# An encoder layer on one core: order of loads and of the first chunks in the front, and of the first two MLP jobs

## What is computed

```
mod = silu(c) @ w_mod + b_mod            # shift1, scale1, gate1, shift2, scale2, gate2
h = rms_norm(x, g_mix) * (1.0 + scale1) + shift1
z = h @ w_in
...                                      # Fourier mixer, gated recurrence, output projection
x = x + gate1 * mix
h = rms_norm(x, g_mlp) * (1.0 + scale2) + shift2
ff = square(relu(h @ w_ff1)) @ w_ff2
x = x + gate2 * ff                       # then a last rms_norm
```

## Time and profile before

| | |
|---|---|
| time, median of 3 runs | 1424.35 us (1422.76 to 1425.23) |
| the profiled execution's own time | 1427.07 us |
| its span, first to last instruction | 1425.3 us |
| TensorE busy | 1392.2 us, 98% of the span |
| TensorE's first matmul | 14.03 us |
| mean granted clock | 0.993 |

### The profile page before, as it was taken

One profiled execution on the slowest core, in us unless ns is written; L12 is line 12 of the kernel. 1 busy time (PEld: TensorE's weight loads), 2 busy tenths in 40 slices (PEclk: granted clock), 3 DMA queues, 4 the chain that ended last, 5 costly groups with the idle time before them and its releaser, 6 DMA issues.

```text
span 1425.3 us, 18554 instructions
## 1 busy us (share of the span) xinstructions
PE 1392.2 (98%) x7594; PEld 1183.4 (83%) x7594; DVE 807.9 (57%) x771; ACT 592.1 (42%) x719; POOL 472.8 (33%) x269
## 2 busy tenths in 40 slices
PE   4999999999999999999999999999999999999998
PEld 2776778898888788888888888888888888888887
DVE  4967688795438954454533454353656434344584
ACT  6667979665335632232222223232332222433241
POOL 0011102135003764565455454532232222233131
PEclk9999999999999999999999999999999999999998
DMA  9443421105310343343343334479997444445542
GB/s 369 161 154 141 133 96 38 45 23 189 143 60 30 111 159 115 121 149 121 139 154 115 126 118 161 158 266 388 377 390 289 148 148 148 162 175 198 203 177 89
DMA packets 75702, 231.31 MB, mean 162 GB/s; under 512 B 5729, under 2 KB 9953, under 8 KB 66786
## 3 DMA queue, kind: packets, MB, share of 16 engines
q1 hardware_dynamic: 75618, 230.12, 44.1%
HBM read 165.09 MB, written 65.01 MB: 161 GB/s over the span
## 4 chain that ended last, share of the span: by engine, by line
PE 53%; issue 2%; POOL 1%; ACT 0%; POOLq 0%
PE bank L785 18%; PE bank L786 18%; PE bank L787 18%; POOL x L2483 0%; ACT w_hi L1579 0%; POOL w_lo L2460 0%; POOL w_s L2436 0%; PE bank L1099 0%; POOL w_lo L2452 0%; PE bank L1092 0%; POOLq L2491 0%; POOL x L2489 0%; POOLq L2488 0%; POOLq L2450 0%
## 5 line engine op out<-in xcount | busy, mean ns | idle before, releaser
L785 PE MATMUL bank<-hin_hi,w_lo 128*128 128x512 f32 (+1 forms) x896 | 302.4, 338 | 0.0
L786 PE MATMUL bank<-hin_lo,w_hi 128*128 128x512 f32 (+1 forms) x896 | 302.0, 337 | 0.0
L787 PE MATMUL bank<-hin_hi,w_hi 128*128 128x512 f32 (+1 forms) x896 | 301.4, 336 | 0.0
L2218 DVE TENSOR_TENSOR hin_lo<-hin,hin_hi 128x3072 fp32r<-128x3072 f32 x28 | 138.9, 4963 | 201.8 <-ACT hin_hi L1591 201.8
L2460 POOL TENSOR_TENSOR w_lo<-w_raw,w_hi 128x2048 fp32r<-128x2048 f32 x28 | 129.6, 4628 | 327.6 <-ACT w_hi L1579 326.1
L785 PEld LDWEIGHTS bank<-hin_hi,w_lo 128*128 128x128 f32 x896 | 170.2, 190 | 18.4 <-issue 0.2
L786 PEld LDWEIGHTS bank<-hin_lo,w_hi 128*128 128x128 f32 x896 | 170.3, 190 | 17.8 <-issue 0.2
L787 PEld LDWEIGHTS bank<-hin_hi,w_hi 128*128 128x128 f32 x896 | 170.1, 190 | 17.8
L1579 ACT ACTIVATE w_hi<-w_raw 128x2048 fp32r<-128x2048 f32 x28 | 53.6, 1916 | 290.3 <-PE bank L787 184.6
L2452 POOL TENSOR_TENSOR w_lo<-w_raw,w_hi 128x512 fp32r<-128x512 f32 x51 | 73.8, 1447 | 200.1 <-ACT w_hi L1517 200.1
L1526 ACT ACTIVATE hid<-bank 128x768 f32<-128x768 f32 (+2 forms) x68 | 52.5, 772 | 163.3 <-PE bank L787 162.5
(11 more groups left out here) (293 smaller groups left out, 3110.8 us busy)
## 6 DMA issues: line engine op xcount, KB each, us to landing
hin<-hid_all SPq DMA_DIRECT2D x28, 1536.0 KB, 6.6
hid_all<-hid SPq DMA_DIRECT2D x105, 384.0 KB, 2.5
w_raw<-in_w_ff SPq DMA_DIRECT2D x36, 1024.0 KB, 8.9
w_raw<-in_w_ff SPq DMA_DIRECT2D x68, 256.0 KB, 2.9
mod_raw<-in_w_mod SPq DMA_DIRECT2D x16, 1024.0 KB, 5.3
x<-in_xT SPq DMA_DIRECT2D x5, 2048.0 KB, 13.4
w_sums<-w_raw SPq DMA_DIRECT2D x8, 1024.0 KB, 14.9
w_raw<-w_sums SPq DMA_DIRECT2D x8, 1024.0 KB, 10.3
```

The costliest lines, as they stand in the source:

```text
L785: pe.matmul(out, w_lo, v_hi, start=first, stop=False, skip_group_check=True)
L786: pe.matmul(out, w_hi, v_lo, start=False, stop=False, skip_group_check=True)
L787: return pe.matmul(out, w_hi, v_hi, start=False, stop=last, skip_group_check=True)
L2218: dve.tensor_tensor(hin_lo[n % 3][:].rearrange("p t n -> p (t n)"), hin[n % 3][:].rearrange("p t n -> p (t n)"), hin_hi[n % 3][:].rearrang ...
```

## The change

In the front, the two w_in tiles and the first modulation quarter are loaded ahead of chunk 1, which now comes in two halves, and the third quarter is loaded ahead of chunk 2. ACT and DVE split the two weight tiles ahead of the root of chunk 0. The squares of chunk 1 move behind `copy_rstd(0)`. TensorE does `front(0, 0)` ahead of everything of chunk 1, and `mod_quarter(2)` behind `front(0, 1)` instead of ahead of it.

In the MLP, two `hid` tiles are exchanged from job 0's last step on (`hid_tile`), so that the copy of P1 of job 1 waits neither for step T1 nor for a store. Steps C22 and C12 of job 0 stand earlier on DVE. The ReLU and square of C12 go from DVE (step B12) to ACT. `split_w1_hi(1, P7)` and `split_w1_hi(1, P3)` stand ahead of `token_hi(P7, 1)` and `token_hi(P4, 1)`.

```diff
+    def hid_tile(j, q):
+
+        if j == S_T4:
+            return hid[S_B11]
+        return hid[S_T4] if j == S_B11 and q else hid[j]
...
-        load_chunk(1)
-        load_first(0)
         sp.dma_start(win_raw[:], w_in_d[TILES[0]]).then_inc(ld_win, 16)
         sp.dma_start(win_raw1[:], w_in_d[TILES[1]]).then_inc(ld_wg, 16)
+        load_first(0)
+        for h, s in enumerate((ld_x[1], ld_x1)):
+            rows = xT_d[h * FT * P:(h + 1) * FT * P, CH:2 * CH]
+            sp.dma_start(x[:, 1, h * FT:(h + 1) * FT, :], rows.rearrange("(k p) n -> p k n", p=P)).then_inc(s, 16)
         load_first(1)
+        load_first(2)
         load_chunk(2)
-        load_first(2)
         load_first(3)
...
         pe.wait_ge(vec_dve, 2)
+        mod_quarter(0)
         norm_spread(0)
-        mod_quarter(0)
         mod_quarter_sum(0)
+        front(0, 0)
         norm_sum(1)
         mod_quarter(1)
         norm_spread(1)
-        front(0, 0)
         mod_quarter_sum(1)
         front(1, 0)
+        front(0, 1)
         mod_quarter(2)
-        front(0, 1)
         mod_quarter_sum(2)
         front(1, 1)
...
             square(0, k)
+        split_win_hi(0)
+        split_win_hi(1)
+        root(0)
+        diagonals(0)
+        mod_copy(0)
+        copy_rstd(0)
         for k in range(2):
             square(1, k)
-        root(0)
-        square(1, 2)
-        diagonals(0)
-        for k in range(3, KD):
+        front_hi(0, 0)
+        for k in range(2, KD):
             square(1, k)
-        split_win_hi(0)
-        split_win_hi(1)
-        mod_copy(0)
-        copy_rstd(0)
         root(1)
-        front_hi(0, 0)
...
             act.wait_ge(ff1_mm, 7 * q + i + 1)
-            after(act, hid_step, NHID * (q - 1) + step)
-            after(act, st_hid[j], 16 * q)
+            if q > 1 or i != P1:
+                after(act, hid_step, NHID * (q - 1) + step)
+                after(act, st_hid[j], 16 * q)
...
         split_w1_hi(1, P6)
         first_relu_square(S_B11, B11, 1)
-        token_hi(P6, 1)
-        split_w1_hi(1, P2)
-        first_relu_square(S_B22, B22, 3)
-        token_hi(P2, 1)
+        first_relu_square(S_T3, B12, 3)
         ff1_out(0, P4, S_B21, T4)
-        token_hi(P3, 1)
         for q in range(1, NJ):
             ff1_out(q, P1, S_B11, T1)
             if q == 1:
+                token_hi(P6, 1)
+                split_w1_hi(1, P2)
+                first_relu_square(S_B22, B22, 5)
+                token_hi(P2, 1)
+                token_hi(P3, 1)
+                split_w1_hi(1, P7)
+                split_w1_hi(1, P3)
                 token_hi(P7, 1)
                 token_hi(P4, 1)
...
         add_squares(0)
-        rstd(0)
-        add_squares(1)
         split_win_lo(0)
         split_win_lo(1)
+        rstd(0)
         mod_quarter_columns(0)
         front_scale(0, 0)
+        add_squares(1, range(1))
+        front_lo(0, 0)
+        add_squares(1, range(1, KD - 1))
         rstd(1)
-        front_lo(0, 0)
...
         token_lo(P1, 1)
+        hid_out(0, C22)
+        hid_out(0, C12)
         token_sum(2, 1)
-        hid_out(0, C22)
         token_lo(P5, 1)
-        for step in (C12, B12, T1):
-            hid_out(0, step)
         token_sum(4, 1)
         token_lo(P6, 1)
-        token_sum(3, 1)
+        hid_out(0, T1)
         token_lo(P2, 1)
         hid_out(0, T3)
+        token_sum(3, 1)
         hid_out(0, T2)
         token_lo(P7, 1)
```

More of the change, by code:

```diff
@@ L371, in build_encoder @@
     ld_x0 = sem("ld_x0_rest")
+    ld_x1 = sem("ld_x1_rest")
     ld_sin = sem("ld_sin")
@@ L641, in store_hid @@
                 if q == 0 and step in (B11, B22):
-                    sp.wait_ge(first_relu, 2 if step == B11 else 4)
+                    sp.wait_ge(first_relu, 2 if step == B11 else 6)
             else:
                 sp.wait_ge(ff1_sq, q + 1)
-            sp.dma_start(hid_d[j, :, pair, c0:c1], hid[j][:, c0:c1]).then_inc(st_hid[j], 16)
+            sp.dma_start(hid_d[j, :, pair, c0:c1], hid_tile(j, q)[:, c0:c1]).then_inc(st_hid[j], 16)
         def w2_freed(m):
@@ L709, in _ @@
                 store_hid(q - 1, S_B21, 0)
-                store_hid(q - 1, S_T4, T4)
+                if q > 1:
+                    store_hid(q - 1, S_T4, T4)
             if q + 1 < NJ:
@@ L714, in _ @@
                 load_w1(q + 1, (A11, A21))
+                if q == 1:
+                    store_hid(0, S_T4, T4)
                 sp.wait_ge(w1_sum, 4 * q + 4)
@@ L1176, in square @@
             if n < NN:
-                act.wait_ge(ld_x0 if c == 0 and k >= FT else ld_x[c], 16)
+                if c < 2 and k >= FT:
+                    act.wait_ge((ld_x0, ld_x1)[c], 16)
+                else:
+                    act.wait_ge(ld_x[c], 16)
             else:
@@ L1523, in ff1_out @@
             act.wait_ge(ff1_mm, 7 * q + i + 1)
-            after(act, hid_step, NHID * (q - 1) + step)
-            after(act, st_hid[j], 16 * q)
-            act.activation(hid[j][:, c0:c1], ps[:, buf + c0:buf + c1], ACT.Relu if i == P4 else ACT.Copy
+            if q > 1 or i != P1:
+                after(act, hid_step, NHID * (q - 1) + step)
+                after(act, st_hid[j], 16 * q)
+            act.activation(hid_tile(j, q)[:, c0:c1], ps[:, buf + c0:buf + c1], ACT.Relu if i == P4 else ACT.Copy
                            ).then_inc(ff1_copy, 1)
@@ L1647, in _ @@
             if q == 1:
+                token_hi(P6, 1)
[5 more added lines that the diff above has]
+                split_w1_hi(1, P3)
                 token_hi(P7, 1)
                 token_hi(P4, 1)
-            split_w1_hi(q, P7)
-            split_w1_hi(q, P3)
+            else:
+                split_w1_hi(q, P7)
+                split_w1_hi(q, P3)
             ff1_out(q, P6, S_T3, T2)
             split_w1_hi(q, P4)
+            if q == 1:
+                ff1_out(q, P7, S_B22, T2)
             if q + 1 < NJ:
@@ L1658, in _ @@
                 split_hin_hi(0)
-            ff1_out(q, P7, S_B22, T2)
+            if q > 1:
+                ff1_out(q, P7, S_B22, T2)
             if q + 1 < NJ:
@@ L2145, in out_of @@
                 return ps[:, 2 * CH * buf + c0:2 * CH * buf + c1]
-            slot, at = hid, NHID * q
+            slot, at = [hid_tile(j, q) for j in range(7)], NHID * q
             if step == U2:
@@ L2169, in hid_out @@
                 if q == 0:
-                    dve.wait_ge(first_relu, 2)
+                    dve.wait_ge(first_relu, 4)
                 after(dve, st_hid[S_T1], 16 * q)
@@ L2175, in hid_out @@
                 if q == 0:
-                    dve.wait_ge(first_relu, 4)
+                    dve.wait_ge(first_relu, 6)
                 m = dve.tensor_tensor(slot[S_T3][:, cols], slot[S_B22][:, cols], slot[S_T3][:, cols], ALU.subtract)
@@ L2183, in hid_out @@
                 dve.wait_ge(ff1_sq, q + 1)
-                after(dve, st_hid[S_T4], 16 * q)
+                if q:
+                    dve.wait_ge(st_hid[S_T4], 16 * q)
+                else:
+                    dve.wait_ge(st_hid[S_B11], 16)
                 m = dve.tensor_tensor(slot[S_T4][:, cols], slot[S_B21][:, cols], slot[S_T2][:, cols], ALU.subtract)
-            m.then_inc(hid_step, 2 if q == 0 and step in (C11, C22) else 1)
+            m.then_inc(hid_step, 2 if q == 0 and step in (C11, C22, C12) else 1)
         def w1_add(q, i):
```

## The result

The changed kernel takes 1428.29 us (median of 15 runs, 1426.24 to 1431.53), the kernel before 1423.70 on the same chip (15 runs, 1422.15 to 1425.76). The ratio is 1.0032, 95% interval 1.0025 to 1.0039: slower by 4.6 us. The profiled execution took 1427.85 us, with a span of 1426.1. Two single runs were slow ones, one of `mlp_copy_first` (3416.73 us) and one of before beside it (2327.06): the ratios leave them out, and they move the printed medians by 0.1 us.

A forecast was written before the change was run, and what follows sets the result against it. TensorE, busy 98% of the span, bounds the kernel; only its idle time and low clock can change. Front +3.4 and MLP -2.4 give +1.0 us on a median of 1424.35: 1425.4, eight in ten within 1421.0 to 1428.6.

The forecast's parts named there:

- Term 1: Front: chunk 2's later landing and quarter 2's uncovered copy delay the sum of chunk 2, +3.4 us (2.3 to 6).
- The idle time ahead of `front(0, 1)`: Front: `front(1, 0)` done at 40.5, `front(0, 1)` starting at 42.1, so TensorE idles 1.6 us.
- The bound from above: Front: up to 6 us lost if idle time brings the low clock back to passes or a quarter on the chain.
- Rival B: Front loses +5.6 us: timed runs of before had less low clock, or new idle time brings it; 1427.6, chance 0.25.
- Term 2: MLP jobs 0 and 1: P7 of job 1 starts at 504.8 instead of 507.2, -2.4 us (0 to -6.5).
- The clock counted as unchanged: MLP: 2.4 us idle ahead of P7, as long as the 2.33 before, so the low clock behind it stays the same.
- Rival A: MLP stretch closes entirely: P7 starts at 502.4, clock stays high, -6.5 us there; 1421.2 in all, chance 0.17.
- Rival C: Front: `front(0, 0)` leads by 7 us and some 4 of them last; 1418, chance 0.06.
- The sum: Whole kernel: +3.4 - 2.4 = +1.0 us on the profiled execution of 1427.07; median forecast 1425.4.

The follow-up runs named there:

- `mlp_copy_first`: MLP half alone on before's front, plus ACT copying P6 of job 1 ahead of two roundings and DVE's T1, T3, T2 one place earlier; 1421.93 us, ratio 0.9971 to before.
- `front_quarter2`: Front half of the change alone, with modulation quarter 2 back ahead of `front(0, 1)`; 1426.46 us, ratio 1.0020 to before.
- `front_only_fill`: Front half of the change alone, with unused matmuls in TensorE's idle time ahead of `front(0, 0)` and `front(1, 0)`; 1429.33 us, ratio 1.0038 to before.
- The second profile: The kernel before, unedited, timed against itself and profiled again; 1425.29 us, ratio 0.9998.
- `mlp_only`: MLP half of the change alone, on the front of before; 1424.22 us, ratio 0.9997 to before.

## Why the prediction was right or wrong

**Term 1, the chain: right in its later steps.** The span after begins its work 0.63 us earlier (13.40 against 14.03). With that shift taken off (without it each forecast is 0.4 to 0.7 us late), the prediction has `front(1, 0)` at 37.0 (measured 37.16), `front(0, 1)` at 41.5 (41.52), quarter 2 at 44.4 (44.35), `front(1, 1)` at 48.3 (48.39) and the sum of chunk 2 at 52.1 (52.11). What it did not have is the half speed of `front(0, 0)` and `front(1, 0)`; the first product of chunk 0 came at 24.78, where it had about 26. The landing of chunk 2 is shown by ACT's first square in ACT's timeline after (it answers to the earlier trace rows):

```profile
37.77 2.19 ACT L1208 ACTIVATE sq<-x 128x512 f32<-128x512 f32 x4 [0.88 <-DMA x<-in_xT]
...
46.34 0.60 ACT L1253 ACTIVATE mod_row<-bank 128x512 f32<-128x512 f32 x1 [3.06 <-PE bank L836]
46.84 1.32 ACT L1261 ACTIVATE hi_f<-x,mod 128x512 fp32r<-128x512 f32 x2
...
504.83 1.06 ACT L1516 ACTIVATE hi_f<-h_f 128x1024 fp32r<-128x1024 f32 x1 [2.09 <-DVE h_f L2115]
505.79 1.04 ACT L1516 ACTIVATE t4b_hi<-t4b_s 128x1024 fp32r<-128x1024 f32 x1
506.74 0.79 ACT L1542 ACTIVATE hid<-bank 128x768 f32<-128x768 f32 x1
```

The forecast less the shift was 37.9. The rows at 46.34 and 46.84 are the uncovered copy and the rounding behind it: ACT waits 3.06 us for quarter 2. `front_quarter2` took that away and won 4.0 us of time, 2.7 by the ratios, and 1.9 in its profile's front.

**The idle time ahead of `front(0, 1)`: wrong.** I had 1.6 us there at the high clock. In the profile after there is none, since `front(1, 0)` ran mostly at 0.50. The bound from above named this case. It cost next to nothing on the chain here: the `lo` of chunk 2 is begun at 40.61, so by my estimate `front(0, 1)` could have started only 0.2 us sooner than its 41.52; `front_only_fill` shows the other side of it, where the clock is high and the wait is 2.14 us.

**Term 1 as a difference: too small.** This is the step that failed. I set the new chain against the one profile of before, whose quarter 1 was at 0.50 and whose front was 35.30 us long, and moved the result to the median of the runs. The second profile has 34.06, so the chain costs 4.7 us against it. Rival B gave exactly this reason, a shorter stretch at the low clock in the timed runs, and its time was 1427.6. The mean clock fits it: 0.994 to 0.996 in the runs of before that the ratios of the experiments use, 0.993 in the profile of before. The median came out at 1428.29, 0.7 above. The two slowest runs of after (1430.79 and 1431.53) have a mean clock of 0.991 against 0.993 for most, but so has one of 1428.30; they have no trace, so what made them slow is not shown.

**Term 2: the mechanism was right, the size only against one form of before.** P5 and P6 no longer wait. From U2 of job 0 to P7 of job 1 the profile before has 23.80 us (483.40 to 507.20), after 21.74 (486.15 to 507.89): 2.06 less, where I had 2.4. Against the other form, in which P7 starts 21.36 us after U2 with the MLP half of before, the changed half is 0.4 us later. I had the earlier trace rows with POOL's 4.83 us before me and took it as an upper bound for the changed kernel; that before itself can run without it, and then has nothing to give, I did not ask. The last three rows of ACT above are the two roundings and the copy of P6 ahead of P7. DVE's timeline after, in the same stretch, which answers to the earlier trace rows:

```profile
498.56 2.31 DVE L2127 TENSOR_TENSOR lo_r<-h_r,hi_r 128x1024 fp32r<-128x1024 f32 x1
500.79 1.77 DVE L2201 TENSOR_TENSOR hid<-hid,hid 128x512 f32<-128x512 f32 x1
502.49 2.30 DVE L2115 TENSOR_TENSOR h_f<-h_r,h_f 128x1024 f32<-128x1024 f32 x1
504.72 1.75 DVE L2204 TENSOR_TENSOR hid<-hid,hid 128x512 f32<-128x512 f32 x1
506.39 1.21 DVE L2127 TENSOR_TENSOR lo_f<-h_f,hi_f 128x1024 fp32r<-128x1024 f32 x1
```

DVE's operations take 2.3 and 1.8 us where they take 1.2 and 0.7 alone: the turns with POOL. `token_sum(3, 1)` ends at 504.79, ACT rounds twice and copies until 507.53, and P7 starts. The profile names `lo_f` as releaser, which ends at 507.60. The two end 0.07 us apart, so that row alone cannot tell which holds P7. `mlp_copy_first` moved both, the copy ahead of `token_sum(3, 1)` and P7's `lo` further back. There P7 starts at 501.97, and its `lo` is made only from 504.06: P7's first part does not need it (its second part waits for it, at 505.43), so in the profile after it was the copy. The Trainium skill, SBUF — State Buffer, section "Who interferes with whom", has the two engines exclude each other for a whole instruction. By that rule the trace agrees in this stretch; the row of 4.83 us in the earlier trace rows, in which POOL got nothing, did not come again in the profile after (its longest pair is 4.70 us for two). It stands in the five profiles of the second form above and in none of the four of the first.

**The clock counted as unchanged: wrong.** That is the second step that failed. I had 2.4 us of idle time ahead of P7; it was 3.12, and behind it the clock was low for 3.4 us in the profile after and 6.8 in `mlp_only`. The two groups of `mlp_only` show the price: the means are 1421.4 us (four runs, high clock) and 1424.7 (seven). Which stretch the faster four had at the high clock has no trace, so that it was this one is inferred from the profile of the other group. The MLP half is worth nothing in the median instead of 2.4 us, and two causes are open for that: the clock took back what the shorter waits gave, or many timed runs of before were of the form in which P7 does not wait. No run here parts them. What `mlp_copy_first` gives is more than either takes: its MLP stretch of 55.50 us lies 1.8 below the shortest of the nine with before's MLP half, and its runs are faster than before's beyond the interval.

**Rival A** (the stretch closes) did not come with this change, as `token_sum(3, 1)` ended at 504.79, 502.0 with the shift of U2 (2.75 us) taken off, and it had to be ready by 499.6. `mlp_copy_first` nearly made it: P7 starts 19.36 us after U2, where the rival had 19.0. **Rival C** did not come at all: the loads did land in order, and though `front(0, 0)` starts at 24.78, ahead of quarter 1 instead of behind it, nothing of that lead is left at the sum of chunk 2.

**The sum.** Predicted +1.0 on the profile and 1425.4 as median. Profile against profile it was +0.8 (1427.85 against 1427.07), which looks like a hit and is none: that profile of before lay above all 15 timed runs of before. Against the second profile it is +3.1 (1424.73), taken beside runs of before that were 2.0 us slower, and in the medians +4.6. That these lie within the range of eight in ten that I gave, up to 1428.6, is owed to rival B and not to the sum.

## What to carry to other kernels

Before a difference is put on a profile, look whether its own time is typical of the timed runs: here 3.4 us of low clock more or less in one execution are worth 1.2 to 1.6 us, more than the +1.0 that I forecast, and a wait of 2.3 us that the change was to remove is missing in four of nine profiles of the same code. A second profile of the kernel before shows the first of the two; here only the profiles of other variants showed the second. An operand that is ready early is worth nothing where a later one of the same chain is the last to come; follow the order of landings to the place where they meet, and check what the moved step had covered. When several short waits are joined to one long one, the idle time may shrink and the time stay, since half speed may follow the long wait; move what stands ahead of the last releaser, as the copy of P6 here.

## What the runs showed of the hardware

Unused matmuls in idle time keep the clock up: with 4.7 us of them in the front the granted clock stayed at 1.00 in the profile, and the front was 2.1 us shorter; in the timed runs the gain is 1.0 us by the ratios, within the noise. They must go into all four groups of 32 columns in turn: 12 matmuls of 512 columns in float32 took 2.78 us so and 10.49 us in one group.

In this kernel short waits sufficed for the clock to fall, but not each time. The idle 2.32 us ahead of `front(1, 0)`, behind a stretch in which quarters and sums left TensorE partly idle, was followed by 0.50 in the profile after. The wait of 2.33 to 2.35 us ahead of P7 of job 1 was followed by it in three profiles and not in two, and one of 0.71 was not. Where the low stretch falls differs from one execution of the same kernel to the next (6.8 or 3.4 us in the front of before), and the runs of `mlp_only` fall in two groups some 3 us apart, with mean clocks of 0.996 or more and 0.994 or less.

DVE and POOL can meet in two ways in the same code. Either they take turns, with 2.31 us for a DVE operation that takes 1.22 alone, or four DVE operations run at their own speed while one of POOL takes 4.83 us. At one meeting in job 1, in nine profiles with the same code there, the first was seen four times and the second five times.
